# Two mixer blocks with expert layers: the last expert's scatter taken apart, the experts' steps reordered, the first buffer refilled by halves

## What is computed

```python
def expert_choice_ffn(h, w_router, w1, w3, w2):          # 16 experts, capacity 32 rows each
    cap = (EC_CAPACITY_FACTOR * T) // N_EXPERTS
    aff = jax.nn.softmax(h @ w_router, axis=-1)
    gate, idx = lax.top_k(jnp.swapaxes(aff, 1, 2), cap)
    xe = h[bidx, idx]                                     # the rows each expert chose
    hid = silu(einsum(xe, w1)) * einsum(xe, w3)           # 1024 -> 1024, twice
    ye = einsum(hid, w2) * gate[..., None]
    return jnp.zeros_like(h).at[bidx, idx].add(ye)

for l in range(2):
    ...
    x = x + g2 * expert_choice_ffn(h2, moe_router[l], moe_w1[l], moe_w3[l], moe_w2[l])
    if l == 0:
        xc = xc + g2c * expert_choice_ffn(hc2, ...)       # layer 0 also for the context
return rms_norm(x, final_norm)
```

## Time and profile before

| | us |
|---|---|
| median of three runs | 1858.9 |
| the profiled execution | 1861.51 |
| its span, first to last instruction | 1859.7 |
| TensorE busy | 1627.1 (87%) |
| VectorE busy | 662.1 (36%) |
| ScalarE busy | 343.1 (18%) |
| GpSimd busy | 44.5 (2%) |
| DMA | 538 MB, mean 289 GB/s |

### The profile page before, as it was taken

The page is one execution under the profiler, slowest core; times in us unless marked ns, Lnnn a source line. Parts: engine busy times, 40 slices in busy tenths (PEclk is TensorE's granted clock), DMA queues, the critical chain, the costliest instruction groups (busy, mean ns, idle before and its releaser), DMA issues.

```text
span 1859.7 us, 23346 instructions
## 1 busy us (share of the span) xinstructions
PE 1627.1 (87%) x9688; PEld 823.8 (44%) x9688; DVE 662.1 (36%) x1438; ACT 343.1 (18%) x848; POOL 44.5 (2%) x41
## 2 busy tenths in 40 slices
PE   6999999999999999899999989899998666666665
PEld 3844674447444654333333333364654333333322
DVE  1267839764343862322322131230543110110202
ACT  2222237412001751100000000021531000000000
POOL 0000200001000000000000000000000000000000
PEclk9999999999999999999999999999999887787887
DMA  9312239874254220999999999931448999999997
GB/s 382 137 46 91 91 136 391 344 307 164 90 196 174 87 96 41 375 428 427 427 427 427 428 427 427 384 132 44 166 203 367 428 426 427 427 428 427 426 427 299
DMA packets 39675, 538.28 MB, mean 289 GB/s; under 512 B 4362, under 2 KB 4874, under 8 KB 6932
## 3 DMA queue, kind: packets, MB, share of 16 engines
q1 hardware_dynamic: 39572, 536.81, 69.5%
HBM read 535.74 MB, written 1.05 MB: 289 GB/s over the span
## 4 chain that ended last, share of the span: by engine, by line
PE 61%; DMA 23%; DVE 6%; SPq 5%; issue 2%; ACT 1%; DVEq 1%; another core or an unknown queue 1%; POOL 0%; POOLq 0%; ACTq 0%
PE bank L646 59%; DMA mem<-in_moe 19%; SPq L2868 5%; PE bank L656 2%; DMA mem<-in_ada_w 2%; DMA mem<-in_w_ada 1%; DVEq L1584 1%; DVE mem L1587 1%; DVE mem L1985 1%; ACT mem L2414 1%; DVE mem L1949 0%; DVE mem L2160 0%; DVE mem L1969 0%; DVE mem L1937 0%
## 5 line engine op out<-in xcount | busy, mean ns | idle before, releaser
L646 PE MATMUL bank<-mem 128*32 128x256 f32 (+15 forms) x8924 | 1515.5, 486 | 209.6 <-DMA mem<-in_moe 120.9
L646 PEld LDWEIGHTS bank<-mem 128*32 128x32 f32 (+5 forms) x8924 | 737.4, 146 | 916.2 <-issue 646.7
L2414 ACT ACTIVATE mem<-bank 128x512 f32<-128x512 f32 (+5 forms) x270 | 133.4, 505 | 1086.8 <-PE bank L646 705.8
L2160 DVE TENSOR_TENSOR mem<-mem,bank 128x512 f32<-128x512 f32 (+1 forms) x32 | 17.8, 556 | 482.4 <-PE bank L646 482.4
L2179 DVE TENSOR_TENSOR mem<-bank,mem 32x512 f32<-32x512 f32 (+1 forms) x120 | 66.7, 555 | 203.4 <-PE bank L646 202.2
L656 PE MATMUL bank<-mem 128*128 128x128 f32 x736 | 119.8, 288 | 14.7 <-DVE mem L2160 5.1
L656 PEld LDWEIGHTS bank<-mem 128*128 128x128 f32 x736 | 82.0, 143 | 100.4 <-issue 55.5
L1774 DVE SCALAR_TENSOR_TENSOR mem<-mem 128x256 f32<-128x256 f32 x160 | 86.9, 543 | 10.4 <-issue 0.9
L1635 DVE SCALAR_TENSOR_TENSOR mem<-mem 128x512 f32<-128x512 f32 x76 | 57.1, 751 | 35.6 <-DMA mem<-in_ada_w 15.2
L2769 POOL TENSOR_TENSOR mem<-mem 128x1 f32<-128x1 f32 (+5 forms) x20 | 16.1, 804 | 1426.8 <-DVE mem L1587 1426.8
L2359 ACT ACTIVATE mem<-bank 128x256 f32<-128x256 f32 (+2 forms) x46 | 16.7, 399 | 127.6 <-PE bank L646 127.5
(11 more groups left out here) (200 smaller groups left out, 568.3 us busy)
## 6 DMA issues: line engine op xcount, KB each, us to landing
mem<-in_moe SPq DMA_DIRECT2D x190, 2048.0 KB, 37.3
mem<-in_ada_w SPq DMA_DIRECT2D x24, 2048.0 KB, 9.5
mem<-in_w_in SPq DMA_DIRECT2D x10, 2048.0 KB, 8.2
mem<-in_w_ada SPq DMA_DIRECT2D x6, 2048.0 KB, 14.3
mem<-in_even_w_in SPq DMA_DIRECT2D x6, 2048.0 KB, 8.6
mem<-in_w_out SPq DMA_DIRECT2D x4, 2048.0 KB, 12.4
mem<-in_odd_w_in SPq DMA_DIRECT2D x3, 2048.0 KB, 8.4
mem<-in_even_w_out SPq DMA_DIRECT2D x2, 2048.0 KB, 9.2
```

Source lines behind the costliest of these rows:

```text
L646: return nc.tensor.matmul(o, lhsT, rhs, start=start, stop=stop, skip_group_check=True)
L2414: took(name, S.activation(o, i, func))
```

## The change

**Order of an expert's steps.** TensorE does `up(e, 0)`, `up(e, 1)`, `gather(e + 1)`, at every fourth expert `scatter` and `slot_rows`, then the transposes `ht`, then `gather_T(e + 1)`, then `down(e)`. VectorE's `modulated(e + 1)` and `one_hot(e + 2)` move behind the sums and the `dgT` work of that expert.

**First buffer by halves.** The first piece that goes into a used buffer (piece 9 in layer 0, 11 in layer 1) is loaded as two halves of 1 MB. The first half waits only until the first two of the four weight tiles of piece 0 are used (`first_half_used`), the second as before.

**Last expert.** Between `up(15, 0)` and `up(15, 1)` TensorE runs `open_totals` and `last_slot_rows`. `open_totals` opens a bank for each of the four 512-column halves of tiles 0 and 1, writes the residual into it with an identity product, and adds the scatter of experts 12 to 14 (a contraction over 96 rows); these four banks stay open. In layer 0 it also scatters experts 12 to 14 to tiles 2 and 3 (four more products), and VectorE adds those to `xres`. `last_slot_rows` (8 products of 256 columns over 16 rows) makes the last expert's slot rows in four groups of 32 partitions; VectorE turns them into `dg_last`. After each half of w2 one VectorE instruction gates all four groups into `y_last`. `last_products` then adds the last expert by products over 32 rows, one per 32-row group: 8 of 512 columns in layer 0; in layer 1 8 of 256 columns in two rounds of four, with a wait between the rounds.

**Norms.** In layer 1 ScalarE squares each half straight from the bank (`half_squares`), the mean is put together from two halves (`final_mean`), and the final scaling reads the banks, by halves; `xres` isn't written in between. In layer 0 ScalarE squares tile 0 from the banks and then copies it to `xres`; VectorE copies the halves of tile 1 and squares each. The adds of tiles 2 and 3 (four) come behind the scaling of tile 0.

```diff
+        SQ_SUM = NORM_SUM[:4] + [v - 2 for v in NORM_SUM[4:]]
...
+                    if 6 * e + j == REFILL[l]:
+                        pe.wait_ge(refill_in[l], 16)
...
+                            if (e, i, kt) == (0, 0, 1):
+                                last.then_inc(first_half_used[l], 1)
...
+                    wait_took(pe, f"bs{l}.L")
+                    for half in range(2):
+                        wait_took(pe, f"y{l}.{e}" + "ab"[half])
+                    last_products()
+
+                totals = {}
+
+                def last_products():
+
+                    if l == 0:
+                        for j in range(T):
+                            for n in range(2):
+                                r0 = 64 * n + 32 * (j // 2)
+                                t = totals[j, n] if j < 2 else B.open(f"sc0.L{j}{n}", "dve")
+                                B.close(t, mm(t.ps[:, :], dg_last[r0:r0 + CAP, P * (j % 2):P * (j % 2) + P], y_last[r0:r0 + CAP, 0:512], j >= 2, True))
+                        return
+                    for k in range(2):
+                        for j in range(2):
+                            for n in range(2):
+                                t = totals[j, n]
+                                q = k ^ j
+                                r0 = 64 * n + 32 * q
+                                last = mm(t.ps[:, SEQ * q:SEQ * q + SEQ], dg_last[r0:r0 + CAP, P * j:P * j + P], y_last[r0:r0 + CAP, 0:SEQ], False, True)
+                                if k == 0:
+                                    last.then_inc(round_done, 1)
+                                else:
+                                    B.close(t, last)
+                        if k == 0:
+                            pe.wait_ge(round_done, 4)
+
+                def open_totals():
+
+                    b = EXPERTS // PER - 1
+                    wait_took(pe, f"sc{l}.{b - 1}{T - 1}1")
                     for s in range(m["streams"]):
-                        wait_took(pe, f"bs{l}.{EXPERTS // PER - 1}{s}")
-                        for half in range(2):
-                            scatter_half(EXPERTS // PER - 1, half, s)
-
-                def scatter_half(b, half, s):
-
-                    if l == 0 and half and s == 0:
-                        pe.wait_ge(y_first, 1)
-                    else:
-                        wait_took(pe, f"y{l}.{EXPERTS - 1}" + "ab"[half])
-                    for j in range(2 * s, 2 * s + 2):
-                        t = B.open(f"sc{l}.{b}{j}{half}", "dve")
-                        y = y_rows[j // 2].rearrange("p (g h c) -> p g h c", g=n_grp, h=2)[:, :, half, :]
-                        B.close(t, mm(t.ps[:, :], dgT[l][:, j // 2, P * (j % 2):P * (j % 2) + P], y, True, True))
+                        wait_took(pe, f"bs{l}.{b}{s}")
+                    wait_took(pe, f"y{l}.{EXPERTS - 2}")
+                    rows = slice(0, CAP * (PER - 1))
+                    for j in range(T):
+                        for n in range(2):
+                            cs = slice(512 * n, 512 * n + 512)
+                            if j < 2:
+                                t = totals[j, n] = B.open(f"sc{l}.L{j}{n}", "act" if l == 0 and j == 0 else "dve")
+                                mm(t.ps[:, :], ident, xres[:, j, cs], True, False)
+                            else:
+                                t = B.open(f"sc{l}.{b}{j}{n}", "dve")
+                            last = mm(t.ps[:, :], dgT[l][rows, j // 2, P * (j % 2):P * (j % 2) + P], y_rows[j // 2][rows, cs], j >= 2, j >= 2)
+                            if j >= 2:
+                                B.close(t, last)
+
+                def last_slot_rows():
+
+                    t = B.open(f"bs{l}.L", "dve")
+                    for half, src in enumerate((sel_e, aff_rows)):
+                        for i in range(4):
+                            r0 = 0 if l else 32 * (i % 2)
+                            c = r0 + EXPERTS - 1
+                            last = mm(t.ps[32 * i:32 * i + 32, SEQ * half:SEQ * half + SEQ], ident[r0:r0 + EXPERTS, c:c + 1].to_broadcast([EXPERTS, CAP]),
+                                      src[r0:r0 + EXPERTS, :], True, True)
+                    B.close(t, last)
...
                 gather_T(0)
                 for e in range(EXPERTS):
                     up(e, 0, "act")
+                    if e == EXPERTS - 1:
+                        open_totals()
+                        last_slot_rows()
+                    up(e, 1, "dve")
                     if e + 1 < EXPERTS:
                         gather(e + 1)
-                    up(e, 1, "dve")
-                    if e + 1 < EXPERTS:
-                        gather_T(e + 1)
                     if e and e % PER == 0:
                         scatter(e // PER - 1)
                     if e % PER == 0:
...
                     for j in range(J):
                         last = tr(t.ps[:, P * j:P * j + P], hid[l][:, P * j:P * j + P])
                     B.close(t, last)
+                    if e + 1 < EXPERTS:
+                        gather_T(e + 1)
                     if e < EXPERTS - 1:
                         down(e)
                     else:
...
+                    if e == EXPERTS - 1:
+                        if l == 0:
+                            sums(EXPERTS // PER - 1, 2)
+                        ps = arrive(dve, f"bs{l}.L")
+                        V.tensor_scalar(dg_last, ps[:, 0:SEQ], C("iota_p"), None, ALU.is_equal)
+                        settle()
+                        took(f"bs{l}.L", V.tensor_tensor(dg_last, dg_last, ps[:, SEQ:2 * SEQ], ALU.mult))
...
-                    if e + 1 < EXPERTS:
-                        modulated(e + 1)
-                    if e + 2 < EXPERTS:
-                        one_hot(e + 2)
...
+                    modulated(e + 1)
+                    if e + 2 < EXPERTS:
+                        one_hot(e + 2)
...
                 e, Wh = EXPERTS - 1, W // 2
-                r0 = CAP * (e % PER)
                 for half in range(2):
                     ps = arrive(dve, f"y{l}.{e}" + "ab"[half])
-                    for k, i in enumerate((0, 2, 1, 3)):
-                        s, h = (i % 2, i // 2) if l == 0 else (0, i)
-                        c = W * h + Wh * half
-                        last = V.tensor_tensor(y_rows[s][r0:r0 + CAP, c:c + Wh], ps[CAP * i:CAP * i + CAP, 0:Wh], gate_ffn[l][CAP * i:CAP * i + CAP, Wh * half:Wh * half + Wh], ALU.mult)
-                        if l == 0 and half and k == 1:
-                            last.then_inc(y_first, 1)
-                    took(f"y{l}.{e}" + "ab"[half], last)
-                for s in range(m["streams"]):
-                    for half in range(2):
-                        for j in range(2 * s, 2 * s + 2):
-                            name = f"sc{l}.{EXPERTS // PER - 1}{j}{half}"
-                            ps = arrive(dve, name)
-                            r = xres[:, j, :].rearrange("p (g h c) -> p g h c", g=n_grp, h=2)[:, :, half, :]
-                            took(name, V.tensor_tensor(r, r, ps.rearrange("p (g c) -> p g c", g=n_grp), ALU.add))
-                            if l == 0 and (j, half) == (3, 0):
-                                mean_of("norm4a", 0, 2)
-                                pow_wait("norm4a")
-                                V.tensor_scalar(xn[:, 0, :], xres[:, 0, :], rstd[:, 0:1], None, ALU.mult).then_inc(xn_done, 1)
-                            if l == 1 and (j, half) == (1, 1):
-                                mean_of("norm6.0", 0, 1)
+                    took(f"y{l}.{e}" + "ab"[half], V.tensor_tensor(y_last[:, Wh * half:Wh * half + Wh], ps[:, 0:Wh], gate_ffn[l][:, Wh * half:Wh * half + Wh], ALU.mult))
+                if l:
+                    return
+                for n in range(2):
+                    ps = arrive(dve, f"sc0.L1{n}")
+                    x = xres[:, 1, 512 * n:512 * n + 512]
+                    took(f"sc0.L1{n}", V.tensor_copy(x, ps[:, :]))
+                    settle()
+                    V.tensor_tensor_reduce(xn[:, 1, 512 * n:512 * n + 512], x, x, 1.0, 0.0, ALU.mult, ALU.add, half_sq[:, 2 + n:3 + n])
+                settle()
+                dve.wait_ge(total_sq, 2)
+                V.tensor_tensor(ssq[:, 0:2], half_sq.rearrange("p (j n) -> p j n", n=2)[:, :, 0], half_sq.rearrange("p (j n) -> p j n", n=2)[:, :, 1], ALU.add)
+                settle()
+                scaled(meansq[:, 0:2], ssq[:, 0:2], 1.0 / D, EPS, ALU.mult, ALU.add).then_inc(ms_done, 1)
+                pow_wait("norm4a")
+                wait_took(dve, "sc0.L01")
+                V.tensor_scalar(xn[:, 0, :], xres[:, 0, :], rstd[:, 0:1], None, ALU.mult).then_inc(xn_done, 1)
+                for j in range(2, 4):
+                    for n in range(2):
+                        name = f"sc0.L{j}{n}"
+                        ps = arrive(dve, name)
+                        r = xres[:, j, 512 * n:512 * n + 512]
```

(41 more changed lines are left out.)

25 lines of the change are left out of this document (14 added, 11 removed).

## The result

| | us |
|---|---|
| changed kernel, median of 6 runs | 1869.24 (1867.71 to 1871.24) |
| kernel before, median of 6 runs beside it | 1861.15 (1857.39 to 1865.12) |
| ratio of the two | 1.0046, interval 1.0033 to 1.0058 |
| the profiled execution | 1871.24, its span 1869.3 |

The change makes the kernel slower by 0.46%, some 8.6 us (the two medians themselves differ by 8.1). I had forecast +4.7 us, with a chance of 0.45 on "within 0.3%" and 0.43 on slower; 1869.24 lies above the range, which ended at 1868.5. Of the 5.6 us between 1869.24 and my 1863.6, 2.3 are the base: I had added to 1858.9, and the kernel before took 1861.15 beside the changed one.

What follows compares the result with a forecast made beforehand. Expert layers were taken as bound by the 427 GB/s weight stream, with serial work behind the last products. Layer 0's +6.8, less 0.6 and 1.45, gave +4.7 us on 1858.9: 1863.6 us, 8-in-10 range 1856.0 to 1868.5.

Steps and rivals of the forecast that it cites:

- The middle of the layers: Experts' new order of steps, both layers: TensorE gains a little per expert, but the weight stream hides it; zero.
- Refill by halves, layer 0: First refill in layer 0: stream starts 1.8 us earlier, 0.6 lost at piece 4's buffer; 1.2 us gained.
- Refill by halves, layer 1: First refill in layer 1: DMA windows short of full rate leave 1.2 us to gain; ends 0 and 1.4.
- Products before w3: Layer 0's last expert: 11.1 us of inserted work, not hidden by idle time before pieces 92 and 93; +5.9 us.
- the idle time there was 4.0 us: Layer 0's last expert, waits before pieces 92 and 93: 4.0 us idle, which can't hide 11.1 us of work.
- Behind w2, layer 0: From w2's end to layer 1's mixer: mean after 6.05 us, four adds delay VectorE's evictions; +0.9 us.
- the clock as a rival: Layer 1's products before w3 run at 1.2 GHz throughout, w2 ends about 9 us late: +13 us; chance 0.08.
- Last expert, layer 1: Up to the last half piece in layer 1: its landing no longer sets the start; -0.6 us left of 1.2.
- The end, layer 1: From the last half piece's start to the last scaling: 8.5 us instead of 9.96, so -1.45 us.
- The sum: Whole kernel: 6.8 for layer 0, -0.6 and -1.45 for layer 1, together +4.7 us.

Runs made afterwards that it cites:

- the kernel with the extra products: Against the changed kernel: six 512-column products that nobody reads, into a free bank, behind layer 0's last products; 1867.63 us, ratio 1.0034 to the kernel before.

## Why the prediction was wrong, step by step

**The middle of the layers: right.** The new order alone is worth nothing (0.9996).

**Refill by halves, layer 0: -1.2 was too much.** The mechanism began as forecast: in all traces where TensorE has its full clock in the first expert, the refill is issued 1.7 us earlier (21.7 against 23.4 from S). But with the new order piece 91 is then used at 435.0 to 436.0, against 435.2 and 435.3 in the two such traces with whole pieces. Nothing of the 1.2 us arrives. The step that failed is that the stream, once started 1.8 us earlier, is held up only at piece 4's buffer. It is held up at piece 1's already, as two rows of SyncE's issues show. The first, of the kernel with all but layer 0's last expert, begins with piece 10; the second, of the kernel before, holds pieces 9 and 10, and its last issue takes 0.33 us, so piece 10 goes out at 771.01:

```profile
768.60 28.81 SPq L3030 DMA_DIRECT2D mem<-in_moe  x8
...
767.58 3.76 SPq L2868 DMA_DIRECT2D mem<-in_moe  x2
```

From S piece 10 goes out at 26.84 and 26.81. Only the 2 MB of the two halves go early; pieces 10 to 13 go out at the same times from S as with the order alone, which has whole pieces (piece 13 at 41.6 in both). At the landing of piece 13 the five traces with the new order, halves and full clock stand at 51.1 to 51.8 from S, the two with whole pieces at 51.6 and 52.0. So some 0.5 us is left of the lead there.

That rest is lost in a scatter of the landings. Pieces land 4.9 us apart, but now and then one comes up to 1.5 us late, and all behind it keep the lateness: in the kernel before pieces 49 and 93 land 6.4 us after the one ahead, in the first trace of all but layer 0's last expert 33 and 77, with the order and layer 1's last expert 48 and 93; in other traces there are more and smaller ones. From piece 13 to piece 91 the thirteen traces take 383.2 to 384.8 us, with halves or without. What causes a late landing no run shows. The Trainium skill ("DMA: Bandwidth & Descriptors", Bandwidth) gives a lower rate for 1 MB than for large transfers, and by it, as I had worked out ahead, the gain would be gone. At piece 91 the traces come out that way, but they give another cause, the issue of piece 10; a lower rate of the halves isn't shown.

**Refill by halves, layer 1: -1.2 was nothing too.** From the first product of layer 1's mixer to the use of the last half piece the traces take 630.4 us with whole pieces (the order alone, layer 1's last expert alone) and 630.3 to 630.4 with halves (the changed kernel and all but layer 0's last expert, twice each). The other traces take up to 2.2 us more; they are of both kinds, the kernel before with 631.7 among them.

**The first expert's clock: missing from the sum.** In the changed kernel's two traces TensorE's clock is 1.2 GHz in the gather and in the first product (0.52 and 0.50 in the windows above, where the kernel with the extra products has 1.00). The first refill then goes out at 23.95 from S, piece 13 lands 1.9 to 2.7 us later than in the traces with halves, new order and full clock, and piece 91 is used 3.1 us later than in them on average (438.65 and 438.53 against 435.5). This isn't tied to a part of the change: the kernel with layer 1's last expert alone has the same two stretches (first refill 26.35, piece 91 at 438.74), and five of the thirteen traces have one or both. The Trainium skill ("TensorE: Matmul & The Clock Gate", Part 1) says that the number of products at the low clock differs from run to run of one kernel. The traces don't show that here, since both pairs of repeats agree. Whether it goes by the kernel or by the execution is open: the profiled execution of the changed kernel lies 2.0 us above its median (1871.24 against 1869.24), that of the last experts alone, with a late refill too, 3.0 below (1868.20 against 1871.18).

**Products before w3: mechanism right, +5.9 should have been +8.7.** The work was sized right (11.2 us against 11.1), the place is as forecast, no transfer is waited for. The term that failed is "the idle time there was 4.0 us". It came from one execution in which piece 93 was one of the late landings. In six of eight traces it is 1.33 + 1.15 = 2.48 us, and 11.2 - 2.5 = 8.7, which is 31.45 - 22.72 of the two traces. My upper end of 8.4 was below it too. The rest of the gap to 5.9 is the refill's 1.2, which I had taken off. This is the step that missed by most: cover read from a single late landing, and a lead of the stream that doesn't reach piece 91.

**Behind w2, layer 0: +0.9 should have been +1.9.** The chain on VectorE was right to 0.2 us (6.23 against 6.05), copies and squares are 0.69 each, and the four adds stand ahead of the evictions with 2.47 us. What I had left out is what TensorE does meanwhile. The change replaces eight products one after another, 6.9 us of work, by 2.0 us of products side by side. The mean comes no sooner for it; all that the longer ones did for the path is that TensorE wasn't idle. It then stands still for 5.77 us, its clock falls to 1.2 GHz, and the transposes on the path take 1.7 us more. I had the clock as a rival only in layer 1, where it did not happen. The extra products put it right, 1.04 us of it.

**Last expert, layer 1: -0.6 was nothing.** It was what I left of the refill's 1.2 us, and that gain isn't there. TensorE still waits for the last half piece, 0.43 us in the changed kernel, and the inserted products are hidden. That I had TensorE setting the start there was wrong by about half a microsecond: 19.66 us from piece 91, of which 0.43 waiting, against my 19.0.

**The end, layer 1: right.** 8.50 us against 8.5.

**The sum.** 8.7 + 1.9 - 1.5 = +9.1, against the measured 8.6 (the interval of the ratio is 6.1 to 10.8). It leaves out what differs by clock and landings. The two profiled executions differ by 9.6 us of span, and there the terms are other ones: -0.2 at S, +3.4 to piece 91, +7.2 to w2's end (the kernel before has the late piece 93), +1.9 to the mixer, -1.3 to the last half piece and -1.4 at the end. For layer 0's last expert alone I find 11.9 us by the ratios where the traces add up to 8.7 + 1.9 = 10.6; the intervals of the two ratios cover the difference.

**What stays open.** With the new order and layer 1's last expert, the halves make 1860.23 into 1857.57, 2.7 us, and the two intervals overlap. That is what a full gain in both layers would give. But the trace without halves is one with the slow clock in the first expert (first refill at 25.08 from S) and the late piece 93, and the pair with the full clock, the order alone against all but layer 0's last expert, shows no gain at piece 91 (435.23 against 435.49 and 435.96). So of the 3.3 us that all but layer 0's last expert gains, the traces account for the 1.5 at the end of layer 1, and the rest is open. I can't tell whether the halves make that clock phase rarer, or the two kernels only fell on different sides of it.

## What to carry to other kernels

Work put in front of a transfer is hidden only up to the idle time that is there in every execution; read that time from several pieces or several traces, because one late landing in one profile made 4.0 us of 2.5 here. A refill that is issued earlier gives nothing unless the next buffers come free earlier too. Products that no result waits for may still hold TensorE's clock for the short work on the path behind them; before they are taken away, look at how long TensorE would stand still and what it must do next. And split a change by layers: the same edit cost 10.6 us where TensorE ends the layer and gave 1.5 us where the last transfer does.

## What the runs showed of the hardware

Eight products over 32 rows and 512 columns, two on each of the four row groups, took 2.02 us. Eight products over 128 rows and the same 512 columns take 8 x 0.88 = 7.0 us one after another, 3.5 times as long. The Trainium skill ("TensorE: Matmul & The Clock Gate", Part 3) gives 3.07 times for four products of 32 rows and 512 columns side by side; the trace, with two in each group, lies somewhat above it. In layer 1 eight of 256 columns in two rounds, with the wait between them, took 1.56 us.

TensorE's clock was still 0.99 in the first 3 us in which it had nothing to do, and 0.50 in the rest of the pause and in all of the transposes behind it. Before, with a pause of 1.1 us in the same place, it stayed at full clock.
